# Whole fp32 products for two pairs at each FFN entry, and forget sums by one scan, in a two-layer hybrid trunk

## The chip, the cores and the metric

The kernel is one program on one core of one Trainium2 chip. The metric is the device time of a launch in microseconds. Before the change it is 2557.03 us, the median of three runs (2553.33 to 2557.09).

## The reference

Two layers, each FFN, mixer, FFN, with an RMS norm before and after each part. 512 rows of a prompt and 8 × 16 rows of samples go through together as 640 tokens of width 1024; the hidden width of an FFN is 2816.

```
h = _rmsnorm(x, g[0]);  gate, up = split(h @ w_in);  x += 0.5 * _rmsnorm((silu(gate) * up) @ w_out, g[1])   # four FFNs
# even mixer, attention branch (8 heads of 64), with a cumulative log forget
logf = log_sigmoid(f_logit + b_f)
c_all = cumsum(concat([flogf_past, logf], axis=1), axis=1)
s = einsum('bqhd,bkhd->bhqk', q, k_all) + c_q[..., None] - c_keys
s = where(causal, s, -1e30);  y = einsum('bhqk,bkhd->bqhd', softmax(s), v_all)
```

The even mixer has a recurrent branch too (a convolution, gates, a linear scan); the odd mixer is differential attention. Everything is fp32.

## The kernel before

**The input projection of an FFN.** The 2816 hidden units are 22 pairs of a gate block and an up block (`KF` = 22). A pair's block is cut in four quarters, and the transposed tokens in four (512 rows of K by 320 tokens), and the product is formed by a seven-product scheme: P1 and P2 take weights as they were loaded, P5, P6, P7 and P3 take sums of quarters (`s1`, `s2`, `s3`, `s4`, formed in place in the weight buffers by VectorE, L624 to L648), and on the token side P5, P6, P7 and P4 take differences T1 to T4 (`dve_t1`, L749, and `dve_t`, L764, written over the tokens' quarters in `xs`). That makes 154 products per FFN. Each is 4 chunks of K.

**The split.** fp32 operands are written as a high and a low part in the rounded format fp32r, and a product is three matmuls per chunk, low × high, high × low, high × high, 12 in all (L933 to L935; for pair 0, L924, L925 and L929, with the low token part last). ScalarE writes a weight quarter's high part (`act_operand`, L604), VectorE the low part (`dve_operand`, L611), into a ring of 5 places (`w_all`) after 4 places of its own (`w_apart`) for an FFN's first products. The seven token matrices are split once per FFN into `xb`, high by ScalarE (L729), low by VectorE (L733).

**What follows a product.** The seven results of a pair are summed in PSUM and by copies: ScalarE copies P1 (L665), then u2 after P6 (L670) and u3 after P7 (L675); VectorE adds P2 (c11, L695), c22 (L698) and c12 after P3; ScalarE makes silu (L682); VectorE multiplies after P4 (hid1, L702) and the upper half at last (hid2). P6 of a pair waits on TensorE for the P1 copy, P7 for u2, P4 for u3, P3 for c22.

**The order.** The table `SEQUENCE` gives the products' order. TensorE walks through it; ScalarE and VectorE walk through the same table in loops over i (`act_ffn`, `dve_ffn`), each step holding a split of product i and what follows product i − 5, so the table sets the order of their queues too. At an FFN's start TensorE holds P1 0, P1 1, P2 0, then transposes of token tile 3, P2 1, tile 4 and so on (`pe_xt`, L1310), while the norm of tiles 3 and 4 (VectorE L1217) is still running. `X_FRONT` says at which steps the later token matrices are split. SP's queue loads the weights (L385): a buffer of pair j + 3 may be overwritten when P3 of pair j has been split (`sp_unit`).

**The forget sums.** `pe_cumulate` (L2208) makes the cumulative sums per row by products with a triangular matrix: 10 fp32 matmuls of 8 columns. In the attention of the prompt, each head's keys need the same sums spread over all rows: `sums(h)` (L1898) does it again with 10 fp32 matmuls of 128 columns. In the profile an fp32 matmul has two records.

## Time and profile before

| | |
|---|---|
| median of three runs | 2557.03 us |
| the profiled execution | 2557.7 us, its span 2555.5 us, granted clock 0.983 |
| busy: TensorE, its weight loads | 95%, 85% |
| busy: VectorE, ScalarE | 66%, 47% |
| busy: GpSimd | 5% |

The page is of one execution. TensorE's busy time is modelled, so it is read by the starts of its instructions rather than by their lengths: in a stream, the distance from one start to the next is the time that one costs. The entries of the four FFNs begin at 20.08, 818.44, 1267.28 and 2107.03 us.

### The profile page before, as it was taken

To read this page: it belongs to the slowest core of one execution; us is meant where nothing else is said; L and a number is where in the kernel's file an instruction comes from. 1 tells how busy PE (TensorE), PEld (TensorE's weight loads), DVE (VectorE), ACT (ScalarE), POOL (GpSimd) and SP (SyncE) were. 2 spreads that over 40 slices of the span, in tenths; PEclk is the share of its full clock that TensorE was granted. 3 is DMA by queue.
4 is the path that set the end of the run, shared out by engine and by line. 5 is a ranking of instruction groups with operands and counts; after the bars stand their busy time and mean duration, and the time that the engine had idled before them with its cause. 6 is when DMAs were issued, how large, how long until landed. Compare 5 with 4: busy or idle time off the path is not lost.

```text
span 2555.5 us, 37705 instructions
## 1 busy us (share of the span) xinstructions
PE 2424.2 (95%) x13907; PEld 2172.0 (85%) x13907; DVE 1694.6 (66%) x2817; ACT 1207.7 (47%) x2243; POOL 121.7 (5%) x177
## 2 busy tenths in 40 slices
PE   6999999999999899999989999999989798999998
PEld 6999987987777899987789998787777577999887
DVE  7777647666666877755687775563236868777546
ACT  5554435344445555434555553453224755545444
POOL 1000001100002000001100000110000010000000
PEclk8999999999999999999999999999997999999999
DMA  5233335421303223334423333343244042333335
GB/s 144 80 88 83 105 126 164 114 72 52 109 24 122 70 83 83 90 125 132 158 73 83 83 88 127 132 149 118 88 124 116 9 140 67 83 91 92 108 128 177
DMA packets 259139, 261.89 MB, mean 102 GB/s; under 512 B 25567, under 2 KB 213999, under 8 KB 258976
## 3 DMA queue, kind: packets, MB, share of 16 engines
q1 hardware_dynamic: 254224, 243.83, 31.9%
q0 software_dynamic: 4464, 14.80, 1.7%
q8 instruction: 102, 1.67, 0.3%
q10 hardware_dynamic: 288, 1.10, 0.1%
q14 instruction: 61, 0.50, 0.1%
HBM read 249.11 MB, written 10.58 MB: 102 GB/s over the span
## 4 chain that ended last, share of the span: by engine, by line
PE 79%; DVE 13%; ACT 3%; issue 3%; DMA 1%; POOL 1%; SPq 0%; DVEq 0%; ACTq 0%; POOLq 0%
PE ps L933 13%; PE ps L935 13%; PE ps L934 13%; PE ps L991 5%; PE ps L992 5%; PE ps L993 5%; PE ps L1420 3%; PE ps L1422 3%; PE ps L1421 3%; PE ps L1050 2%; PE ps L1052 2%; PE ps L1051 2%; DVE w_all L611 1%; DVE xb L733 1%; DVE small L2033 1%
## 5 line engine op out<-in xcount | busy, mean ns | idle before, releaser
L933 PE MATMUL ps<-xb,w_all 128*128 128x320 f32 x2320 | 722.2, 311 | 24.0 <-DVE arena L702 11.2
L934 PE MATMUL ps<-xb,w_all 128*128 128x320 f32 x2320 | 720.0, 310 | 0.0
L935 PE MATMUL ps<-xb,w_all 128*128 128x320 f32 x2320 | 719.9, 310 | 0.0
L933 PEld LDWEIGHTS ps<-xb,w_all 128*128 128x128 f32 x2320 | 438.8, 189 | 29.4 <-DVE w_all L611 16.9
L511 DVE TENSOR_TENSOR w_all<-raw,w_all 128x1024 fp32r<-128x1024 f32 (+1 forms) x204 | 208.1, 1020 | 364.2 <-ACT w_all L521 196.9
L934 PEld LDWEIGHTS ps<-xb,w_all 128*128 128x128 f32 x2320 | 438.6, 189 | 0.0
L935 PEld LDWEIGHTS ps<-xb,w_all 128*128 128x128 f32 x2320 | 438.3, 189 | 0.0
L505 ACT ACTIVATE w_all<-raw 128x1024 fp32r<-128x1024 f32 (+1 forms) x204 | 182.5, 895 | 442.2 <-PE ps L993 237.5
L611 DVE TENSOR_TENSOR w_all<-raw,w_all 128x512 fp32r<-128x512 f32 x404 | 278.1, 690 | 150.6 <-ACT w_all L604 149.8
L604 ACT ACTIVATE w_all<-raw 128x512 fp32r<-128x512 f32 x404 | 253.6, 629 | 197.4 <-PE ps L935 134.8
L991 PE MATMUL ps<-w_all 128*128 128x512 f32 x528 | 205.9, 390 | 0.9 <-DVE w_all L526 0.9
L992 PE MATMUL ps<-w_all 128*128 128x512 f32 x528 | 205.5, 389 | 0.0
L993 PE MATMUL ps<-w_all 128*128 128x512 f32 x528 | 205.4, 389 | 0.0
L611 DVE TENSOR_TENSOR w_all<-gain,w_all 128x512 fp32r<-128x512 f32 x196 | 135.0, 690 | 70.3 <-ACT w_all L604 69.7
L604 ACT ACTIVATE w_all<-gain 128x512 fp32r<-128x512 f32 x196 | 122.9, 629 | 87.8 <-PE ps L935 68.1
L1420 PE MATMUL ps<-w_all,xT_lo 128*128 128x512 f32 x354 | 142.1, 401 | 14.8 <-ACT tok L1488 8.3
L1421 PE MATMUL ps<-w_all,xT_hi 128*128 128x512 f32 x354 | 138.2, 390 | 0.0
L1422 PE MATMUL ps<-w_all,xT_hi 128*128 128x512 f32 x354 | 138.0, 390 | 0.0
L991 PEld LDWEIGHTS ps<-w_all 128*128 128x128 f32 x528 | 99.1, 188 | 23.2 <-DVE w_all L526 2.6
L993 PEld LDWEIGHTS ps<-w_all 128*128 128x128 f32 x528 | 99.1, 188 | 20.7
L992 PEld LDWEIGHTS ps<-w_all 128*128 128x128 f32 x528 | 99.1, 188 | 20.1
L1420 PEld LDWEIGHTS ps<-w_all,xT_lo 128*128 128x128 f32 x354 | 66.6, 188 | 37.6 <-DVE w_all L511 17.2
(375 smaller groups left out, 4075.2 us busy)
## 6 DMA issues: line engine op xcount, KB each, us to landing
raw<-in_w_ffn_out SPq DMA_DIRECT2D x176, 512.0 KB, 3.3
raw<-in_w_ffn_in SPq DMA_DIRECT2D x120, 512.0 KB, 5.1
gain<-in_w_ffn_in SPq DMA_DIRECT2D x56, 512.0 KB, 4.3
raw<-in_w_in_odd SPq DMA_DIRECT2D x56, 256.0 KB, 2.7
raw<-in_w_out_even SPq DMA_DIRECT2D x16, 512.0 KB, 3.4
raw<-in_w_out_odd SPq DMA_DIRECT2D x16, 512.0 KB, 3.5
gain<-in_norm_g POOLq DMA_DIRECT2D x12, 512.0 KB, 6.3
raw<-in_w_in_even SPq DMA_DIRECT2D x24, 256.0 KB, 2.7
```

Source lines behind the costliest of these rows:

```text
L511: return nc.vector.tensor_tensor(lo, raw[:, RAW[u][0], 0:n], hi.bitcast(F32), ALU.subtract)
L604: nc.scalar.activation(w_ring(i)[0], operand_raw(f, name, j), ACT.Copy).then_inc(op_hi, 1)
L611: nc.vector.tensor_tensor(lo, operand_raw(f, name, j), hi.bitcast(F32), ALU.subtract).then_inc(op_lo, 1)
L933: nc.tensor.matmul(dst, wl, xh[:, k, :], start=fresh and k == 0, stop=False, skip_group_check=True)
L934: nc.tensor.matmul(dst, wh, xl[:, k, :], start=False, stop=False, skip_group_check=True)
L935: mm = nc.tensor.matmul(dst, wh, xh[:, k, :], start=False, stop=(k == HK - 1), skip_group_check=True)
L991: nc.tensor.matmul(dst, xl, wh[:, cols], start=start, stop=False)
L992: nc.tensor.matmul(dst, xh, wl[:, cols], start=False, stop=False)
L993: mm = nc.tensor.matmul(dst, xh, wh[:, cols], start=False, stop=stop)
L1420: nc.tensor.matmul(dst, xl, wh, start=(k == 0), stop=False)
L1421: nc.tensor.matmul(dst, xh, wl, start=False, stop=False)
L1422: return nc.tensor.matmul(dst, xh, wh, start=False, stop=(k == KD - 1))
```

## The change

**Whole products (the FFNs).** `WHOLE = 2`: the 14 products of pairs 0 and 1 in each FFN are plain fp32 matmuls, one per chunk, with the weight buffers and the token quarters as they are. They wait for the loaded weights, the sums and the T's themselves (`pe_whole_ready`) rather than for splits. The T's are written into the low places of `xb` as fp32 (`xb_f32`), so they no longer go over the tokens; s2 of the two pairs is written to two places of the ring (`whole_s2`). The splits of T1 to T4 and B22, which pair 2 and the rest need, move to steps 14 to 21. `SEQUENCE` has a new beginning (26 products, the same from P1 of pair 4 on), the transposes of tiles 3 and 4 stand together before P2 of pair 1, pair 0's first sums go between the norms of tiles 3 and 4, and the weight buffers of pairs 0 and 1 come free with the product P3 itself.

**Forget sums (the even mixer).** Four transposes put the negated log forgets of all heads as 8 rows of 512 into PSUM, VectorE makes one scan along them (`c_rows`), four transposes turn it back for the row sums, and `sums(h)` is one fp32 product of 512 columns that spreads row h to all 128 rows.

```diff
-SEQUENCE = [("P1", 0), ("P1", 1), ("P2", 0), ("P2", 1), ("P1", 2), ("P2", 2)]
-SEQUENCE += [(name, j) for name in ("P5", "P6", "P7", "P4", "P3") for j in range(2)]
-SEQUENCE += [("P5", 2), ("P1", 3), ("P6", 2), ("P2", 3), ("P7", 2), ("P5", 3), ("P4", 2), ("P6", 3), ("P3", 2), ("P7", 3)]
-SEQUENCE += [(name, j - back) for j in range(4, KF + 1)
+SEQUENCE = [("P1", 0), ("P2", 0), ("P1", 1), ("P2", 1), ("P5", 0), ("P1", 2), ("P6", 0), ("P2", 2), ("P7", 0), ("P5", 1)]
+SEQUENCE += [("P4", 0), ("P6", 1), ("P3", 0), ("P7", 1), ("P5", 2), ("P4", 1), ("P6", 2), ("P3", 1), ("P7", 2)]
+SEQUENCE += [(name, j - back) for j in range(3, KF + 1)
              for name, back in (("P1", 0), ("P5", 0), ("P4", 1), ("P6", 0), ("P2", 0), ("P3", 1), ("P7", 0))
              if j - back < KF]
...
+WHOLE = 2
+SPLIT = [i for i, (_, j) in enumerate(SEQUENCE) if j >= WHOLE]
...
+                i = PLACE["P3", (prev - UNITS["A%d" % f]) // 2]
+                if i in SPLIT_NO:
+                    sp.wait_ge(op_lo, split_count(f, i))
+                else:
+                    sp.wait_ge(prod_mm, NPROD * f + i + 1)
...
 
             a11, a12, a21, a22 = quarters(f, j)
             g = KF * f + j
-            dve.wait_ge(op_lo, NPROD * f + PLACE["P1", j] + 1)
+            operand_free(dve, f, "P1", j)
             pair_wait(dve, f, j, 1)
             nc.vector.tensor_tensor(a11, a11, a21, ALU.subtract).then_inc(s3_done, 1)
...
         def dve_sums(dve, f, i):
 
             name, j = SEQUENCE[i]
...
-            if (name, j) == ("P4", 1):
-                dve_first_sums(dve, f, 2)
-            if name == "P1" and j >= 3:
+            if name == "P1" and j > WHOLE:
                 dve_first_sums(dve, f, j)
-            if name == "P5" and j >= 2:
+            if name == "P5" and j >= WHOLE:
                 dve_s2(dve, f, j)
-            if name == ("P7" if j < 2 else "P5" if j < 4 else "P2"):
-                dve.wait_ge(op_lo, NPROD * f + PLACE["P2", j] + 1)
-                dve.wait_ge(s2_done, KF * f + j + 1)
-                nc.vector.tensor_tensor(a12, a12, a21, ALU.subtract).then_inc(s4_done, 1)
+            if j >= WHOLE and name == ("P5" if j == WHOLE else "P2"):
+                dve_s4(dve, f, j)
 
```

The token matrices, the loops and the products:

```diff
+        def x_whole(name):
+
+            return xb_f32[:, XB[name] + 1] if name in T_NO else xs_quarter(*XB_AT[name])
 
         def act_xb(act, f, name):
...
         def dve_xb(dve, f, name):
+
+            if name in T_NO:
+                dve.wait_ge(prod_mm, done_of(f, {x: p for p, x in XOF.items()}[name], WHOLE - 1))
             dve.wait_ge(xb_hi_done, 7 * f + XB_ORDER.index(name) + 1)
-            nc.vector.tensor_tensor(xb[:, XB[name] + 1], xs_quarter(*XB_AT[name]), xb[:, XB[name]].bitcast(F32),
+            nc.vector.tensor_tensor(xb[:, XB[name] + 1], x_whole(name), xb[:, XB[name]].bitcast(F32),
                                     ALU.subtract).then_inc(xb_lo_done, 1)
 
         def dve_t1(dve, f, t):
...
+            t1 = nc.vector.tensor_tensor(x_whole("T1")[:, :, c0:c1], b12, xs[:, 0:HK, c0:c1], ALU.subtract)
             if t == NT - 1:
...
-            nc.vector.tensor_tensor(xs_quarter(*out), xs_quarter(*plus), xs_quarter(*minus),
-                                    ALU.subtract).then_inc(t_add, 1)
+                dve.wait_ge(t_add, 4 * f + T_NO["T2"])
+            nc.vector.tensor_tensor(x_whole(name), plus, minus, ALU.subtract).then_inc(t_add, 1)
...
         def dve_first_t(dve, f):
 
-            dve_first_sums(dve, f, 0)
-            dve_t1(dve, f, 2)
-            dve_t1(dve, f, 3)
-            dve_operand(dve, f, 4)
-            dve_operand(dve, f, 5)
-            dve_t1(dve, f, 4)
-            dve_operand(dve, f, 6)
-            dve_first_sums(dve, f, 1)
-            dve_xb(dve, f, "T1")
-            dve_t(dve, f, "T3")
-            dve_operand(dve, f, 7)
-            dve_t(dve, f, "T2")
+            for t in range(2, NT):
+                dve_t1(dve, f, t)
 
         FFN_A = ["A0", "A1", "A2", "A3"]
...
         THIRD_LATE = PLACE["P4", 0] + RING + 1
-        X_FRONT = {8: "T2", 10: "T3", 12: "T4", 14: "B22"}
...
                     dve_xb(dve, f, X_FRONT[i])
-                if 7 < i < NPROD:
+                if i in SPLIT_NO:
                     dve_operand(dve, f, i)
-                if i in (6, 7):
-                    dve_s2(dve, f, i - 6)
-                elif 9 < i < NPROD:
                     dve_sums(dve, f, i)
+                if i == 5:
+                    dve_t(dve, f, "T2")
+                if i == 6:
+                    dve_s2(dve, f, 0)
+                if i == 7:
+                    dve_t(dve, f, "T3")
+                if i == 8:
+                    dve_first_sums(dve, f, 1)
+                    dve_s2(dve, f, 1)
                 if i == 9:
                     dve_t(dve, f, "T4")
+                    dve_s4(dve, f, 0)
+                if i == 11:
+                    dve_s4(dve, f, 1)
+                if i == 13:
+                    dve_first_sums(dve, f, WHOLE)
                 if 0 <= i - RING < NPROD and i - RING != THIRD[1]:
...
 
+        def pe_whole_ready(pe, f, name, j):
+
+            g = KF * f + j
+            if name in ("P1", "P2"):
+                pair_wait(pe, f, j, 0)
+            elif name == "P4":
+                pair_wait(pe, f, j, 1)
+            else:
+                pe.wait_ge({"P5": s1_done, "P6": s2_done, "P7": s3_done, "P3": s4_done}[name], g + 1)
+            if XOF[name] in T_NO:
...
-                if i == AHEAD - 1:
+                if i == PLACE["P2", 1]:
                     pe_xt(pe, pre_, 3, 3)
-                if i == AHEAD:
                     pe_xt(pe, pre_, 4, 4)
-
-                    pe.wait_ge(xt_hi, XT[pre_] + 4)
-                if i == AHEAD + 2:
+                if i == PLACE["P5", 0]:
                     pe.wait_ge(xt_hi, XT[pre_] + NT)
-                pe.wait_ge(op_lo, NPROD * f + i + 1)
-                if j == 0:
-                    pe.wait_ge(xb_hi_done, 7 * f + XB_ORDER.index(XOF[name]) + 1)
+                if j < WHOLE:
+                    pe_whole_ready(pe, f, name, j)
+                else:
+                    pe.wait_ge(op_lo, split_count(f, i))
...
                 dst = bank({"P2": b2, "P5": b5, "P3": b5}.get(name, b1), HT)
-                hi, lo = w_ring(i)
...
-                if j == 0:
-
+                if j < WHOLE:
+                    w = whole_s2(j) if name == "P6" else operand_raw(f, name, j)
                     for k in range(HK):
-                        wh, wl = hi[:, k * P:(k + 1) * P], lo[:, k * P:(k + 1) * P]
-                        nc.tensor.matmul(dst, wl, xh[:, k, :], start=fresh and k == 0, stop=False, skip_group_check=True)
-                        nc.tensor.matmul(dst, wh, xh[:, k, :], start=False, stop=False, skip_group_check=True)
-                    pe.wait_ge(xb_lo_done, 7 * f + XB_ORDER.index(XOF[name]) + 1)
-                    for k in range(HK):
-                        wh = hi[:, k * P:(k + 1) * P]
-                        mm = nc.tensor.matmul(dst, wh, xl[:, k, :], start=False, stop=(k == HK - 1), skip_group_check=True)
```

The entry's norms, and the forget sums:

```diff
             f = FFN_PRE.get("pre%d" % (p + 1))
-            if f is not None:
-                for i in range(2):
-                    dve_operand(dve, f, i)
-            elif nxt:
+            if nxt:
                 for i in range(2):
...
             if f is None and nxt:
...
-            if f is not None:
-                dve_operand(dve, f, 3)
             pre(dve, p, 3)
             if f is None:
                 dve_lo(dve, nxt[0] + 3, None, nxt[1]).then_inc(lo_done, 1)
+            else:
+                dve_first_sums(dve, f, 0)
             pre(dve, p, 4)
...
                     pe.wait_ge(nc_done, h)
-                for kb in range(NP):
-                    for b in range(kb + 1):
-                        mm = nc.tensor.matmul(bank(6, P, kb * P), lgn[:, b, h:h + 1].to_broadcast([P, P]),
-                                              con[:, C_UT:C_UT + P] if b == kb else ones,
-                                              start=(b == 0), stop=(b == kb))
-                mm.then_inc(nc_mm, 1)
+                nc.tensor.matmul(bank(6), con[0:NH, C_ID + h:C_ID + h + 1].to_broadcast([NH, P]), c_rows,
+                                 start=True, stop=True).then_inc(nc_mm, 1)
...
             for i in range(NP):
-                for b in range(i + 1):
-                    mm = nc.tensor.matmul(bank(7, NH, 64 + i * NH), con[:, C_UT:C_UT + P] if b == i else ones,
-                                          lgf[:, b, :], start=(b == 0), stop=(b == i))
+                mm = nc.tensor.transpose(ps[0:NH, 7, i * P:(i + 1) * P], lgn[:, i, :], ident)
+            mm.then_inc(lg_ps, 1)
+
+        def pe_cumulate_turn(pe):
+            pe.wait_ge(cum_done, 1)
+            for i in range(NP):
+                mm = nc.tensor.transpose(bank(7, NH, 64 + i * NH), c_rows[:, i * P:(i + 1) * P],
+                                         con[0:NH, C_ID:C_ID + NH])
             mm.then_inc(cq_mm, 1)
 
...
+                pe_cumulate_turn(pe)
...
                 if m == K_AT + 2:
-                    dve.wait_ge(cq_mm, 1)
-                    nc.vector.tensor_copy(cq, bank(7, NP * NH, 64).rearrange("p (t h) -> p t h", h=NH)).then_inc(cq_done, 1)
+                    dve.wait_ge(lg_ps, 1)
+                    nc.vector.tensor_tensor_scan(c_rows, con[0:NH, C_ONE:C_ONE + 1].to_broadcast([NH, SEQ]),
+                                                 ps[0:NH, 7, :], 0.0, ALU.mult, ALU.add).then_inc(cum_done, 1)
...
                     dve_sample_prepare(dve, 0)
+            dve.wait_ge(cq_mm, 1)
+            nc.vector.tensor_scalar(cq, bank(7, NP * NH, 64).rearrange("p (t h) -> p t h", h=NH),
```

The following rows are the order of instructions on an engine: line, operation, written from read, and what it waits for. Lines of the changed kernel have moved: L611 is L637 there, L604 L630, L665 L701, L670 L706, L675 L711, L682 L718, L764 L801, L749 L789, L695 L731, L1898 L1920.

VectorE at the first FFN's entry, before, from the first sums of pair 0 on (`op_hi` is a split's high part, `xt_hi` a transposed token tile, `t_add` a finished T):

```order
L624 TENSOR_TENSOR raw<-raw 128x512 [waits raw_in2,op_lo]
L626 TENSOR_TENSOR raw<-raw 128x512 [waits s3_done]
L749 TENSOR_TENSOR arena<-arena 128x4x64 [waits xt_hi,xb_lo_done]
L749 TENSOR_TENSOR arena<-arena 128x4x128 [waits xt_hi]
L611 TENSOR_TENSOR w_all<-gain,w_all 128x512 [waits op_hi] x2
L749 TENSOR_TENSOR arena<-ps,arena 128x4x128 [waits xt_ps]
L611 TENSOR_TENSOR w_all<-raw,w_all 128x512 [waits op_hi]
L624 TENSOR_TENSOR raw<-raw 128x512 [waits raw_in3,op_lo]
L626 TENSOR_TENSOR raw<-raw 128x512 [waits s3_done]
L733 TENSOR_TENSOR xb<-arena,xb 128x1280 [waits xb_hi_done]
L764 TENSOR_TENSOR arena<-arena 128x4x320 [waits xt_hi,t_add]
L611 TENSOR_TENSOR w_all<-raw,w_all 128x512 [waits op_hi]
```

The same place in the changed kernel; its first sums of pair 0 (L657, L659) stand ahead of it:

```order
L789 TENSOR_TENSOR xb_f_50<-arena 128x4x64 [waits xt_hi]
L789 TENSOR_TENSOR xb_f_50<-arena 128x4x128 [waits xt_hi]
L789 TENSOR_TENSOR xb_f_50<-ps,arena 128x4x128 [waits xt_ps]
L637 TENSOR_TENSOR w_apart<-gain,w_apart 128x512 [waits op_hi]
L801 TENSOR_TENSOR xb_f_50<-arena,xb_f_50 128x1280 [waits t_add,xt_hi]
L667 TENSOR_TENSOR w_f_58<-raw 128x512 [waits s3_done]
L731 TENSOR_TENSOR scratch<-scratch,ps 128x320 [waits prod_mm,p1_done]
L637 TENSOR_TENSOR w_apart<-gain,w_apart 128x512 [waits op_hi]
L801 TENSOR_TENSOR xb_f_50<-arena 128x1280
L657 TENSOR_TENSOR raw<-raw 128x512 [waits raw_in3,prod_mm]
L659 TENSOR_TENSOR raw<-raw 128x512 [waits s3_done]
L667 TENSOR_TENSOR w_f_58<-raw 128x512 [waits s3_done]
```

The split of T1 (L733) and the splits of the ring's first places are gone from between the T's, s2 and the c11 sum stand where they were, and pair 1's first sums come after T3.

ScalarE at the same place before, from the first silu (L682) to u2 of pair 0 (L670), after the copies of P1:

```order
L682 ACT_TABLE_LOAD
L682 ACTIVATE scratch<-scratch 128x320 [waits c11_done]
L729 ACTIVATE xb<-arena 128x1280 [waits t_add]
L604 ACTIVATE w_all<-raw 128x512 [waits prod_mm,s3_done]
L682 ACTIVATE scratch<-scratch 128x320 [waits c11_done]
L604 ACTIVATE w_all<-raw 128x512 [waits prod_mm,s3_done]
L729 ACTIVATE xb<-arena 128x1280 [waits t_add]
L604 ACTIVATE w_all<-raw 128x512 [waits prod_mm,raw_in2]
L670 ACTIVATE scratch<-ps 128x320 [waits prod_mm]
```

And changed, from the copy of P1 of pair 0 (L701) to u2 and u3 of pair 0 (L706, L711):

```order
L701 ACTIVATE scratch<-ps 128x320 [waits prod_mm]
L630 ACTIVATE w_apart<-gain 128x512 [waits raw_in4]
L701 ACTIVATE scratch<-ps 128x320 [waits prod_mm]
L630 ACTIVATE w_apart<-gain 128x512 [waits raw_in4]
L718 ACT_TABLE_LOAD
L718 ACTIVATE scratch<-scratch 128x320 [waits c11_done] x2
L706 ACTIVATE scratch<-ps 128x320 [waits prod_mm]
L711 ACTIVATE arena<-ps 128x320 [waits prod_mm]
```

Pair 0's u2 copy (L706) stood behind both silu and the splits between them; now it stands right behind the two silu, which wait for c11 of pairs 0 and 1, and no split stands between.

TensorE in the prompt's attention before, around the sums of the second head (`nc_done` is the copy of the sums before them, `s_read` the reading of a score block):

```order
L1919 MATMUL ps<-arena 128x384 [waits hl_copied]
L1898 MATMUL ps<-con,arena 128x128 [waits nc_done]
L1898 MATMUL ps<-con,arena 128x128 x9
L1694 MATMUL ps<-con,scratch 128x128 [waits sn_done]
L1694 MATMUL ps<-con,scratch 128x128 x3
L1919 MATMUL ps<-arena 128x512 [waits s_read]
```

And changed:

```order
L1939 MATMUL ps<-arena 128x384 [waits hl_copied]
L1920 MATMUL ps<-arena,con 128x512 [waits nc_done]
L1718 MATMUL ps<-con,scratch 128x128 [waits sn_done]
L1718 MATMUL ps<-con,scratch 128x128 x3
L1939 MATMUL ps<-arena 128x512 [waits s_read]
```

The ten matmuls of 128 columns are one of 512; nothing else moved.

## Rows read from the trace of the kernel before

**Rows 1.** The page: the chain that ended last, share of the span by engine.

```profile
PE 79%; DVE 13%; ACT 3%; issue 3%; DMA 1%; POOL 1%; SPq 0%; DVEq 0%; ACTq 0%; POOLq 0%
```

**Rows 2.** Timeline of PE (start, us): first product, P1 of pair 4, by FFN.

```profile
20.08 0.60 PE L924 MATMUL ps<-xb,w_apart 128*128 128x320 f32 x1 [0.82 <-ACT xb L729]
...
83.25 0.31 PE L933 MATMUL ps<-xb,w_all 128*128 128x320 f32 x1
...
818.44 0.31 PE L924 MATMUL ps<-xb,w_apart 128*128 128x320 f32 x1
...
882.37 0.31 PE L933 MATMUL ps<-xb,w_all 128*128 128x320 f32 x1
...
1267.28 0.30 PE L924 MATMUL ps<-xb,w_apart 128*128 128x320 f32 x1
...
1330.07 0.31 PE L933 MATMUL ps<-xb,w_all 128*128 128x320 f32 x1
...
2107.03 0.30 PE L924 MATMUL ps<-xb,w_apart 128*128 128x320 f32 x1
...
2170.08 0.31 PE L933 MATMUL ps<-xb,w_all 128*128 128x320 f32 x1
```

**Rows 3.** Timeline of PE: two successive steady products' first matmuls.

```profile
150.13 0.31 PE L933 MATMUL ps<-xb,w_all 128*128 128x320 f32 x1
...
151.89 0.31 PE L933 MATMUL ps<-xb,w_all 128*128 128x320 f32 x1
```

**Rows 4.** Timeline of PE: the longest waits of the second FFN's entry.

```profile
842.53 0.42 PE L924 MATMUL ps<-xb,w_all 128*128 128x320 f32 x1 [2.99 <-DVE w_all L611]
...
864.92 0.38 PE L933 MATMUL ps<-xb,w_all 128*128 128x320 f32 x1 [2.87 <-DVE arena L702]
```

**Rows 5.** Timeline of PE: fp32 matmuls of the even mixer.

```profile
543.92 1.02 PE L2281 MATMUL ps<-arena 128*128 128x512 f32 x2
...
544.78 0.38 PE L2282 MATMUL ps<-arena 128*128 128x128 f32 x2
```

**Rows 6.** Weight loads of a product (busy us, mean ns, idle before).

```profile
L933 PEld LDWEIGHTS ps<-xb,w_all 128*128 128x128 f32 x2320 | 438.8, 189 | 29.4 <-DVE w_all L611 16.9 <-issue 12.5
```

**Rows 7.** Windows: length, busy (count) of PE PEld DVE ACT POOL, PEclk.

```profile
43.00:50.00 7.00, 6.52 (x26) 6.53 (x27) 7.00 (x10) 6.99 (x11) 0.00 (x0) 0.53 0.00 1
```

**Rows 8.** Groups by form in 813 to 865: VectorE, then ScalarE.

```profile
L611 DVE TENSOR_TENSOR w_all<-raw,w_all 128x512 fp32r<-128x512 f32 x12 | 8.0, 684 | 1.4 <-ACT w_all L604 1.4
...
L604 ACT ACTIVATE w_all<-raw 128x512 fp32r<-128x512 f32 x13 | 8.0, 623 | 5.7 <-DMA raw<-in_w_ffn_in 5.6
```

**Rows 9.** Timeline of PE and VectorE: tiles 3 and 4 of the second FFN.

```profile
826.12 1.09 PE L1310 MATMUL ps<-con,tok 128*128 128x128 f32 x8 [0.95 <-DVE tok L1217]
...
826.97 0.39 PE L933 MATMUL ps<-xb,w_apart 128*128 128x320 f32 x1
...
826.78 1.28 DVE L1217 SCALAR_TENSOR_TENSOR tok<-x,small,gain 128x1024 f32<-128x1024 f32 x1 [0.72 <-POOL small L1186]
```

**Rows 10.** Timeline of SP's queue: pair 3's weights of the second FFN.

```profile
854.66 4.07 SPq L385 DMA_DIRECT2D raw<-in_w_ffn_in  x4
```

**Rows 11.** Timeline of PE: first head's sums; a later head of the loop.

```profile
677.94 3.86 PE L1898 MATMUL ps<-con,arena 128*128 128x128 f32 x20
...
702.80 2.50 PE L1898 MATMUL ps<-con,arena 128*128 128x128 f32 x20
...
706.28 1.12 PE L1919 MATMUL ps<-arena 64*128 64x512 f32 x2
...
711.84 0.82 PE L1898 MATMUL ps<-con,arena 128*128 128x128 f32 x5
```

**Rows 12.** Windows (columns as in rows 7): eight heads of the attention loop.

```profile
684.30:756.00 71.70, 69.77 (x446) 52.72 (x444) 51.10 (x158) 36.07 (x102) 0.00 (x0) 1.00 0.03 9
```

**Rows 13.** Groups by form in 600 to 640: old cumulate; recurrence scan.

```profile
L2208 PE MATMUL ps<-small,con 128*128 128x8 f32 x20 | 2.3, 252 | 0.0
...
L2393 DVE TENSOR_TENSOR_SCAN att<-att 128x640 f32<-128x640 f32 x1 | 1.5, 1492 | 0.0
```

More of the change, by code:

```diff
@@ L130 @@
 PLACE = {key: i for i, key in enumerate(SEQUENCE)}
+WHOLE = 2
+SPLIT = [i for i, (_, j) in enumerate(SEQUENCE) if j >= WHOLE]
+SPLIT_NO = {i: n for n, i in enumerate(SPLIT)}
+NSPLIT = len(SPLIT)
 RING, AHEAD = 5, 4
@@ L178, in build_trunk @@
         att = at_byte("att", 0, [P, 3456], back=4 * (W_ALL - 4 * BW))
+        w_f32 = at_byte("w_f32", 0, [P, W_ALL], back=4 * W_ALL)
         gain = at_byte("gain", 8 * D, [P, 2, D])
@@ L371, in build_trunk, with split_count @@
         O_BANK = [0, 1, 4, 3, 2]
+        def split_count(f, i):
+            return NSPLIT * f + SPLIT_NO[i] + 1
         def sp_unit(sp, u, it, src):
@@ L1146, in act_norm_rest @@
             sq_m(act, p, 4)
-            if f is not None:
-                for i in range(2, AHEAD):
-                    act_operand(act, f, i)
             if p == 5:
@@ L1164, in act_norm_start @@
                 sq_x(act, -1, t)
-            act_operand(act, 0, 0)
             for t in TILES[0]:
                 act_xt(act, "pre0", t, t)
-            act_xb_first(act, -1)
-            for i in range(1, AHEAD):
-                act_operand(act, 0, i)
             for t in TILES[1]:
                 sq_x(act, -1, t)
+            act_xb_first(act, -1)
             act.wait_ge(lam_sum, 1)
@@ L1243, in dve_norm_rest @@
             f = FFN_PRE.get("pre%d" % (p + 1))
-            if f is not None:
-                for i in range(2):
-                    dve_operand(dve, f, i)
-            elif nxt:
+            if nxt:
                 for i in range(2):
@@ L1252, in dve_norm_rest @@
             post_gain(dve, p, 4)
-            if f is not None:
-                dve_operand(dve, f, 2)
             if f is None and nxt:
@@ L1259, in dve_norm_rest @@
                 return
-            if f is not None:
-                dve_operand(dve, f, 3)
             pre(dve, p, 3)
@@ L1276, in dve_norm_start @@
                 pre(dve, -1, t)
-            dve_operand(dve, 0, 0)
-            dve_xb_first(dve, -1)
-            for i in range(1, AHEAD):
-                dve_operand(dve, 0, i)
             dve.wait_ge(par_in, 16 * 9)
```

83 lines of the change are left out of this document (52 added, 31 removed).

## The prediction

> **What bounds the kernel now.** I began with the chain of work that ended last: TensorE carries most of it and VectorE is a distant second [rows 1]. So a time is won where TensorE stops or where it is given fewer columns, and I looked for its stops. The timeline of TensorE through the four FFNs shows two regimes. In the steady one a product of the input projection takes 151.89 − 150.13 = 1.76 us with nothing between products [rows 3]; nothing the change does to VectorE or ScalarE can help there. In the entry it is otherwise. From the first product to the start of P1 of pair 4 lie 26 products, which would take 26 × 1.76 = 45.8 us, and the rows give 63.17, 63.93, 62.79 and 63.05 us, 252.9 in all and 63.2 in the mean [rows 2]. Two groups of eight transposes belong there (826.97 − 826.12 = 0.85 each [rows 9]), 1.7. The remaining 15.7 us of each entry are waits and stretches at a low clock: four times that, 63 us, is all that the FFN part can draw on. The longest waits are 2.99 us for an operand split by VectorE (L611) and 2.87 us for a multiplication of VectorE (L702) [rows 4]: TensorE waits for its preparers.
>
> **What a whole fp32 product costs.** The trace has no whole product in the FFN, but it has fp32 matmuls in the even mixer: two records of 512 columns (L2281) start at 543.92 and the next line at 544.78, so 0.43 us a record [rows 5]. Per column that is 0.84 ns, and 320 columns take 0.27. A whole product has 4 chunks of 2 records: 8 × 0.27 = 2.15 us, against 1.76 for the 12 split matmuls. The change thus makes 14 products per FFN longer by 0.39, 5.5 us per FFN, 22 in four. This is the price; the rest must be earned by waits that go.
>
> What can make a record longer is its weight load. A load takes 189 ns [rows 6], and 12 of them, 2.27 us, are more than the 1.76 of a product [rows 3]; so loads lie beside the matmuls before them. A 0.27 us record has more room for its load than a 0.147 us one, and I add nothing. The Trainium skill speaks against that: "TensorE: Matmul & The Clock Gate", Part 3, "The mechanism", says a weight load overlaps running matmuls only where it goes to another row group, and every load here takes all 128 rows. By that rule a record would take 0.46, a product 3.67; the rows just named do not bear the rule out, so it gets a small chance among the rivals.
>
> **What the entry gives back.** Per FFN, 14 splits go on ScalarE (0.62 each) and 14 on VectorE (0.68 each) [rows 8]: 18 us of preparing, in queues that serve a TensorE that waits. The splits of T1 to T4 and of B22 don't go, they move behind the first 14 places; T1 can be used as soon as it is written. So the 2.99 us stop, whose last link was a split, has no place any more. The 2.87 us stop stands at the end of a transfer: SP issues pair 3's weights at 854.66, they take 4.07 us to land [rows 10], the first sums of pair 3 stand on them in VectorE's queue and L702 stands behind these. The new order has P3 of pair 0 as product 12 instead of 14, and the buffer is freed by the product itself. I put that issue at 850.3 in the second FFN, so the weights land about 854.4, while P1 of pair 3 comes at place 19, about 863. That stop goes too.
>
> What is late next I worked out by laying the second FFN out, each engine's queue in the order shown ahead, with durations of the rows. Three stops remain.
> - Transposes of token tile 4. Both late tiles are now transposed before P2 of pair 1. TensorE is through three whole products at 818.44 + 3 × 2.15 = 824.9 and through tile 3 at 825.8. Tile 4 is normalised by VectorE from 826.78 to 828.06 now [rows 9]; four splits (2.7 us) leave the queue ahead of it, and pair 0's two first sums (1.4, of a split's shape) enter, so it is done about 827.5: a wait of 1.7.
> - P7 of pair 0 needs the copy of P6's result (u2). On ScalarE this copy stands behind both silu of pairs 0 and 1, as it did, and the second waits for VectorE's sum after P2 of pair 1, which comes late in that engine's queue, about 838.5, behind T3 and the first sums of pair 1. The copy is done at 839.5, TensorE there 1.2 earlier.
> - P7 of pair 2 needs a copy that waits for the last hidden block of pair 0, VectorE's at 861.0: a wait of 1.3.
>
> Together 4.2 us. The entry is then 14 × 2.15 + 12 × 1.76 + 1.7 + 4.2 = 57.1 instead of 63.2, a gain of 6.1 and **24.5 us** in four FFNs (5.6 in the first, where the first products run at the low clock and the whole products pay double for it, but start 1.0 earlier as they wait for no split; 6.7, 6.3 and 5.9 in the others). Its bounds: with no stop left the gain is 4 × 10.3 = 41; with every stop of before still there it is a loss of 22, the price alone. I stay near the first end since the two longest stops have links that are simply no longer there.
>
> The clock enters here too. In the first FFN from 43 to 50 us the granted clock is 0.53, the lower level of 1.2 GHz, and 26 matmuls fill 6.52 us [rows 7], after a stop of 3 us. At that level a whole product would be 4.3 us. Fewer long stops before means fewer such stretches; I book no extra gain for it, since the sum already ran at full pitch save in the first FFN.
>
> **The forget sums.** In the prompt's attention each head begins with 20 records of 128 columns (L1898): 2.50 us, and 3.86 for the first head [rows 11]. The new product has one row set of 8 partitions against 512 columns, two records; a 512-column fp32 product of this same loop takes 1.12 [rows 11]. Saved are 1.38 per head, 7 heads 9.7, and 2.7 for the first: 12.4 if all of it falls on the stream. In the loop TensorE is busy 69.77 of 71.70 us and VectorE 51.10, ScalarE 36.07 [rows 12], so TensorE sets the pace, but a head of 711.84 − 702.80 = 9.04 us will come down to 7.8 with some 6.4 of VectorE in it (51.10 / 71.70 of 9.04), and the chain of scores, exponent, transposes has less slack. I take **11**, the lower end being only the first head's 2.7, where the loop comes to be set by that chain.
>
> The other half is a wash. The 20 records of the old cumulate (2.3 us busy [rows 13]) go; 4 transposes come in their place and 4 later, each time half of the 0.85 for eight [rows 9], and one scan over 512 columns on VectorE: the scan in the recurrence takes 1.49 for 640 [rows 13], so about 1.2. It lies beside the projection's matmuls, with the transposes back at the start of the Q part, many microseconds on. At worst TensorE waits there for the scan, 1.2; at best it saves 1.4. I take 0.
>
> **The sum.** 2557.0 − 24.5 − 11 = 2521.5. The profiled run of before took 2557.7 (its span is 2555.5), 0.7 over the median, so differences from its rows stand on the median unscaled. Forecast **2522**.
>
> **Rivals.**
> - *The stops return* (0.20). VectorE and ScalarE are in-order queues, and some ten operations change places on each. If one late link costs each entry 3.5 us more (a u2 copy behind a silu, first sums behind a transfer, a low-clock stretch at 4.3 per product for two products), the FFN part is 10: 2557 − 10 − 11 = 2536. For it: two of my three remaining stops hang on such copies. Against it: their total work has fallen by 18 us per entry.
> - *The attention loop isn't TensorE's* (0.10). If the chain between engines sets a head's 9.04 us, only the first head's gain stays: 2557 − 24.5 − 2.7 = 2530. For it: the loop has waits between every two engines. Against it: 97% busy at a granted clock of 1.00 [rows 12].
> - *Weight loads are laid bare* (0.04), the slower end. If the 189 ns load of a whole record can't be hidden (fp32 weights, unlike the split ones), a record is 0.27 + 0.19 = 0.46, a product 3.67, and 56 products cost 85 us more than in my sum. The longer products would swallow the 4 × 4.2 = 17 of stops, so the time is 2522 + 85 − 17 = 2590. It decides from 35 us more, that is 2.15 + 35 / 56 = 2.8 us per whole product, 0.35 a record. Against it: rows 3 and 6 above, and the 0.43 per record in rows 5, which is no more than twice the pitch of a split matmul scaled to 512 columns (1.76 / 12 × 1.6 × 2 = 0.47, from rows 3) and leaves room for no bare load.
> - *Nothing much* (0.04): the FFN part at 0 from stops and clock together and the loop kept by its chain, 2557 − 2.7 = 2554.
>
> **How the numbers follow.** The forecast has 0.62, the rest above 0.38. Its own range is 2510 to 2531 (waits 1.5 to 6 per entry, attention 9 to 12). The range for 8 in 10 reaches on the fast side to all stops gone with the whole of the forget sums, 2557 − 41 − 12.4 = 2504, and on the slow side to the first rival and a little of the second with it, 2543. A measurement of this kernel tells 0.2%, about 5 us, from no change. Faster: forecast and the first two rivals, 0.92; within 0.2%: 0.04; slower: 0.04.
>
> **What would show it.** A whole product in the trace after should start 2.15 us before the next, its records 0.27 apart. The four entries, first product to P1 of pair 4, should be 56 to 58 us, with stops at the tile 4 transposes and before P7 of pairs 0 and 2, and none near 3 us. A head of the attention loop should be 7.8 us. An entry above 60 says the stops returned, a product above 2.8 that the loads are bare, a head still at 9 that another chain sets the loop. The prediction is wrong if whole products run at the lower clock for several pairs, as then each costs 4.3 and ten of them eat the FFN gain.

## The result

The changed kernel takes 2564.28 us (median of six runs, 2561.65 to 2567.31) where the kernel before takes 2555.31 (six runs): a ratio of 1.0033, with an interval of 1.0022 to 1.0045. It is slower by 9.0 us, little but clear of the noise; a gain of 35 us was forecast. The profiled run, the fastest of the six, has a span of 2559.7 us, 4.2 more than the profiled run of before; the trace can account for these 4.2 only.

The FFN entries did what the prediction said. On the timeline of TensorE in the changed kernel, the first whole product and the start of P1 of pair 4 in each FFN (start, us, engine, line, operation, count), answering to [rows 2]:

```profile
18.86 0.54 PE L966 MATMUL ps<-arena,raw 128*128 128x320 f32 x1
...
77.00 0.31 PE L973 MATMUL ps<-xb,w_all 128*128 128x320 f32 x1
...
841.36 0.43 PE L966 MATMUL ps<-arena,raw 128*128 128x320 f32 x1
...
898.24 0.31 PE L973 MATMUL ps<-xb,w_all 128*128 128x320 f32 x1
...
1283.11 0.43 PE L966 MATMUL ps<-arena,raw 128*128 128x320 f32 x1
...
1339.97 0.31 PE L973 MATMUL ps<-xb,w_all 128*128 128x320 f32 x1
...
2117.30 0.43 PE L966 MATMUL ps<-arena,raw 128*128 128x320 f32 x1
...
2174.29 0.31 PE L973 MATMUL ps<-xb,w_all 128*128 128x320 f32 x1
```

The entries are 58.14, 56.88, 56.86 and 56.99 us, 228.9 together: 24.1 less than the 252.9 of before. And yet the second FFN begins at 841.36 instead of 818.44. The loss lies between the first FFN's entry and that start. The same timeline at the loop over the heads, the spread of the sums (L1920) of four of its heads, answering to [rows 11]:

```profile
676.85 1.12 PE L1920 MATMUL ps<-arena,con 8*128 8x512 f32 x2
...
684.29 1.12 PE L1920 MATMUL ps<-arena,con 8*128 8x512 f32 x2
...
697.10 2.07 PE L1920 MATMUL ps<-arena,con 8*128 8x512 f32 x2
...
711.28 2.07 PE L1920 MATMUL ps<-arena,con 8*128 8x512 f32 x2
```

From the second head's sums to the third's it is 684.29 − 676.85 = 7.44 us. That can't be held against the 7.8 of the forecast, which was for a steady head: the same step took 8.42 us before, and only the next ones 9.04.

```profile
685.34 2.50 PE L1898 MATMUL ps<-con,arena 128*128 128x128 f32 x20
...
693.76 2.50 PE L1898 MATMUL ps<-con,arena 128*128 128x128 f32 x20
```

Then a head of the changed kernel takes 711.28 − 697.10 = 14.18, and the two records that took 1.12 take 2.07. The windows say why (length, busy time and count of TensorE, weight loads, VectorE, ScalarE and GpSimd, then the granted clock and DMA), first of before, then of after:

```profile
680.00:760.00 80.00, 78.06 (x485) 59.59 (x484) 54.23 (x165) 38.22 (x106) 1.46 (x3) 0.99 0.08 31
```

```profile
680.00:760.00 80.00, 79.33 (x231) 48.26 (x230) 40.17 (x120) 29.48 (x81) 0.00 (x0) 0.54 0.02 7
...
690.00:700.00 10.00, 10.00 (x29) 6.19 (x29) 5.59 (x18) 2.77 (x8) 0.00 (x0) 0.50 0.00 0
...
700.00:710.00 10.00, 10.00 (x34) 7.15 (x34) 4.89 (x13) 5.09 (x12) 0.00 (x0) 0.50 0.01 2
```

The page shows it at a glance, in the row of the granted clock in 40 slices of 64 us (tenths), at the eleventh and twelfth:

```profile
PEclk9999999999759999999999999999998999999999
```

TensorE is busy all the time, more than before, but with 231 matmuls in the 80 us where there were 485 (in part by the change itself, as a head has 18 records fewer): its granted clock is 0.50 from about 686 on, the lower of its two levels (1.2 GHz), and was 0.99. VectorE and ScalarE, by contrast, have become idler. And no long stop goes ahead of the fall: the longest wait of TensorE in the ten us before it is 0.48 us.

```profile
682.86 0.66 PE L1979 MATMUL ps<-arena,att 128*128 128x64 f32 x4 [0.48 <-ACT att L2008]
```

From the first head's sums to the second FFN it is 172.29 us (841.36 − 669.07) against 140.50 before, 31.8 us lost where 11 were to be won. So the books are: 24.1 won in the entries, 1.2 by the earlier start of the first one, 2.6 between P1 of pair 4 of the first FFN and the loop, 31.8 lost in the loop and behind it, the rest within 0.4: 4.2 slower.

### The profile page after: what moved, and what is told of

Its sections match the earlier page's. It is cut to its first block, busy times and chain, and to the rows that moved or that the text cites. A ratio compares the mean times of both kernels' runs of the same rounds, so it can differ in the third digit from the quotient of the medians.

```text
span 2559.7 us, 36785 instructions
## 1 busy us (share of the span) xinstructions
PE 2456.5 (96%) x13527; PEld 2151.1 (84%) x13527; DVE 1666.6 (65%) x2762; ACT 1180.7 (46%) x2187; POOL 118.5 (5%) x177
## 4 chain that ended last, share of the span: by engine, by line
PE 82%; DVE 11%; ACT 3%; issue 2%; DMA 1%; POOL 1%; ACTq 0%; SPq 0%; DVEq 0%
PE ps L973 13%; PE ps L974 13%; PE ps L975 13%; PE ps L1031 5%; PE ps L1033 5%; PE ps L1032 5%; PE ps L1444 3%; PE ps L1446 3%; PE ps L1445 3%; PE ps L1090 2%; PE ps L1092 2%; PE ps L1091 2%; PE ps L966 2%; PE ps L1939 1%; PE ps L1979 1%
## 5 line engine op out<-in xcount | busy, mean ns | idle before, releaser
L973 PE MATMUL ps<-xb,w_all 128*128 128x320 f32 x2176 | 672.9, 309 | 9.2 <-ACT scratch L706 6.7
L974 PE MATMUL ps<-xb,w_all 128*128 128x320 f32 x2176 | 672.4, 309 | 0.0
L975 PE MATMUL ps<-xb,w_all 128*128 128x320 f32 x2176 | 672.4, 309 | 0.0
L973 PEld LDWEIGHTS ps<-xb,w_all 128*128 128x128 f32 x2176 | 408.4, 188 | 12.0 <-issue 12.0
L974 PEld LDWEIGHTS ps<-xb,w_all 128*128 128x128 f32 x2176 | 408.4, 188 | 0.0
L975 PEld LDWEIGHTS ps<-xb,w_all 128*128 128x128 f32 x2176 | 408.4, 188 | 0.0
L637 DVE TENSOR_TENSOR w_all<-raw,w_all 128x512 fp32r<-128x512 f32 x364 | 251.6, 691 | 144.4 <-ACT w_all L630 143.5
L630 ACT ACTIVATE w_all<-raw 128x512 fp32r<-128x512 f32 x364 | 229.2, 630 | 182.4 <-PE ps L975 138.0
L637 DVE TENSOR_TENSOR w_all<-gain,w_all 128x512 fp32r<-128x512 f32 x180 | 124.4, 691 | 65.3 <-ACT w_all L630 64.9
L630 ACT ACTIVATE w_all<-gain 128x512 fp32r<-128x512 f32 x180 | 113.4, 630 | 84.1 <-PE ps L975 66.2
```

What stands on the lines that cost most here:

```text
L630: nc.scalar.activation(w_ring(i)[0], operand_raw(f, name, j), ACT.Copy).then_inc(op_hi, 1)
L637: nc.vector.tensor_tensor(lo, operand_raw(f, name, j), hi.bitcast(F32), ALU.subtract).then_inc(op_lo, 1)
L973: nc.tensor.matmul(dst, wl, xh[:, k, :], start=fresh and k == 0, stop=False, skip_group_check=True)
L974: nc.tensor.matmul(dst, wh, xl[:, k, :], start=False, stop=False, skip_group_check=True)
L975: mm = nc.tensor.matmul(dst, wh, xh[:, k, :], start=False, stop=(k == HK - 1), skip_group_check=True)
```

## Theories

**R**: the clock fell because of the form of the new sums, which put data on 8 of the array's 128 rows where the old ones filled all. **W**: it fell because a head has less matmul work, whatever its form. **S**: it fell by the way the loop is entered (scan and transposes, an earlier start). **H**: the level that the first heads get is kept to the end.

## The two parts by themselves

The FFN part alone, the forget sums as they were:

```diff
-                nc.tensor.matmul(bank(6), con[0:NH, C_ID + h:C_ID + h + 1].to_broadcast([NH, P]), c_rows,
-                                 start=True, stop=True).then_inc(nc_mm, 1)
+                for kb in range(NP):
+                    for b in range(kb + 1):
+                        mm = nc.tensor.matmul(bank(6, P, kb * P), lgn[:, b, h:h + 1].to_broadcast([P, P]),
+                                              con[:, C_UT:C_UT + P] if b == kb else ones,
+                                              start=(b == 0), stop=(b == kb))
+                mm.then_inc(nc_mm, 1)
...
```

> The FFN part alone; the forget sums are as before (20 records of 128 columns per head, old cumulate). The trace after shows the four entries 24.0 us shorter and the attention loop of the even mixer at half the clock. If the loss lies in the sums alone, the loop keeps a granted clock of 1.00 and 9.04 us a head, and the time is 2555 - 24 = 2531 us. If the shorter entries themselves cost something elsewhere, it is above 2540.

2530.62 us (2528.24 to 2531.05), a ratio of 0.9898 (0.9881 to 0.9914): 25.7 us won against the 2556.31 that the kernel before took beside it, as expected. The loop's window in that run, at 9.04 us a head, shows the upper level:

```profile
700.00:710.00 10.00, 10.00 (x65) 7.54 (x63) 7.21 (x20) 5.81 (x15) 0.00 (x0) 1.00 0.15 52
```

The forget part alone, on the FFNs of before:

> The forget part alone, the FFNs as before. If the loss lies in it, the loop runs at a granted clock near 0.5 with about 14.2 us a head, and the time is 2555 + 29 = 2584 us. If the loop fell to the low clock only because it starts some 9 us earlier behind the new FFN entry, the clock here stays at 1.00 and the time is about 2543.

2591.08 us (2587.23 to 2591.94), 1.0138 (1.0121 to 1.0155): 34.8 us lost, where 29 were expected, with the loop low as in the changed kernel. So the entries, and the start that they move, have no part in it. The two parts add up to the whole: 34.8 − 25.7 = 9.1 us, and 9.0 were measured.

```profile
696.00:716.00 20.00, 20.00 (x59) 12.46 (x57) 9.89 (x30) 7.02 (x20) 0.00 (x0) 0.50 0.00 0
```

Then the forget part was split in its turn: sums as before, the scan and its transposes kept.

> The changed kernel with each head's sums as before (20 records of 128 columns); the scan and the two groups of four transposes stay. It prices the cumulate part, which the prediction put at 0 between -1.4 and +1.2. Between the first FFN's entry and the loop the trace of after is 2.8 us shorter than before, so theory R expects the loop at 1.00 with 9.04 us a head and 2530.6 - 2.8 = 2528 us. Theory S (the scan and its transposes bring the loop in at the low clock) expects 0.5 and above 2560.

2530.65 us (2529.06 to 2531.55), the same as without the scan. Theory S falls, and so does the 2.8 us that the two traces had seemed to show for the scan: the first head's sums start at 671.92 here and at 671.97 in the FFN part alone. The loop's start moves by as much without a cause in the program: two kernels below, with the changed kernel's instructions up to the loop, enter it at 671.28 and 671.91, and the changed kernel at 669.07. So the 2.6 us of the books can't be put down to the change either. The scan took 1.20 us on VectorE and its transposes 0.6 and 0.4 us busy, and they are worth what they cost.

## Rows or work

One difference to the changed kernel: the selector and the sums take all 128 rows. Rows 8 to 127 meet zeros of the selector, so the sums are the same.

```diff
-                nc.tensor.matmul(bank(6), con[0:NH, C_ID + h:C_ID + h + 1].to_broadcast([NH, P]), c_rows,
+                nc.tensor.matmul(bank(6), con[:, C_ID + h:C_ID + h + 1].to_broadcast([P, P]), c_all,
```

> The changed kernel with one difference: the product that spreads a head's sums takes all 128 rows of the array (the selector's other rows are zero) instead of 8, still 512 columns and two records. Theory R (the clock fell since the sums no longer fill the array's rows): the loop is granted 1.00, a head takes about 7.5 us, and the time is 2564 - 44 = 2520 us. Theory W (it fell since a head has fewer matmul columns and instructions) and theory S (it fell by the way the loop is entered, whatever the sums look like): 0.5 as in the changed kernel, 14.2 us a head, 2564.

2524.94 us (2524.74 to 2525.84), 0.9879 (0.9863 to 0.9896): 39 us faster than the changed kernel, by rows that add nothing to the result, and 5.7 faster than the FFN part alone. The second and the third head still take 8.63 and 9.62 us, then the clock is back. A later head, from its sums to the next, and three windows:

```profile
695.82 1.12 PE L1921 MATMUL ps<-arena,con 128*128 128x512 f32 x2
...
703.49 1.12 PE L1921 MATMUL ps<-arena,con 128*128 128x512 f32 x2
```

```profile
680.00:690.00 10.00, 9.18 (x31) 5.62 (x30) 6.41 (x21) 4.70 (x14) 0.00 (x0) 0.68 0.00 0
...
690.00:700.00 10.00, 10.00 (x53) 6.48 (x52) 7.31 (x23) 5.62 (x17) 0.00 (x0) 0.98 0.00 1
...
700.00:710.00 10.00, 9.78 (x50) 6.20 (x49) 8.44 (x26) 5.70 (x15) 0.00 (x0) 1.00 0.16 54
```

A head is then 703.49 − 695.82 = 7.67 us (the next takes 8.71 at 1.00, with waits for ScalarE). What rows 8 to 127 bring to the product are gate weights left there by the recurrent branch, so this run doesn't tell filled rows from the numbers in them. The opposite edit keeps the 8 rows and restores the work, by issuing each head's sums three times:

```diff
+                for again in range(3):
+                    mm = nc.tensor.matmul(bank(6), con[0:NH, C_ID + h:C_ID + h + 1].to_broadcast([NH, P]), c_rows,
+                                          start=True, stop=True)
```

> The changed kernel with each head's sums issued three times over, on 8 rows: 6 records of 512 columns, 2.6 us at the full clock, as long on TensorE as the 20 records of before. Theory R: the loop stays near 0.5 and each head gets 4 more records of about 1 us, 18 us a head, time 2564 + 29 = 2593. Theory W: the clock is back at 1.00, a head 9.2 us, time 2534. Theory S: as theory R.

2590.83 us (2589.94 to 2592.11). After its second head the loop is at 0.50 again, to about 814 us:

```profile
716.00:736.00 20.00, 20.00 (x52) 11.14 (x50) 7.66 (x21) 5.68 (x14) 0.00 (x0) 0.50 0.08 26
```

So theory W, as put, falls too: as long on TensorE as before, but on 8 rows, it is no help; as short as in the changed kernel, but on 128 rows, it is.

A third kernel made only 2 of the 8-row product's 512 columns for heads 2 to 7, which then add stale sums.

> The changed kernel without the spread of the sums for heads 2 to 7: only 2 of the 512 columns are made, so these heads add stale sums. It asks whether the 8-row product itself takes the clock down or whether it is the filled rows of before that are missed. If they are missed: 0.5 as in the changed kernel, about 12.2 us a head, 2564 - 6 x 2 = 2552 us. If the 8-row product is the brake: 1.00, about 6.6 us a head, 2564 - 6 x 7.6 = 2518.

2554.49 us in the median, but the seven runs lie in two groups, 2538.68 to 2542.27 and 2554.49 to 2557.30. The profiled one, of the lower group, held 1.00 for two heads longer than the changed kernel and then fell:

```profile
690.00:700.00 10.00, 10.00 (x61) 7.20 (x60) 8.85 (x30) 6.18 (x18) 0.00 (x0) 1.00 0.00 0
...
710.00:720.00 10.00, 10.00 (x33) 6.83 (x33) 4.87 (x15) 3.65 (x10) 0.00 (x0) 0.50 0.00 0
```

So the loop falls without the 8-row product too: something of the old sums is missed, whatever the new product does. The upper group lies near the 2552 that was expected for that case. Whether the 8-row product pulls the clock down besides is not shown: the lower group would fit that, but the next runs fall at different heads with 128-row products as well.

## Does the level follow the rows at once?

Heads 0 to 3 on 128 rows and heads 4 to 7 on 8, and the reverse (`few = h < 4`):

```diff
+                few = h >= 4
+                sel = con[0:NH if few else P, C_ID + h:C_ID + h + 1].to_broadcast([NH if few else P, P])
+                nc.tensor.matmul(bank(6), sel, c_rows if few else c_all, start=True, stop=True).then_inc(nc_mm, 1)
```

> The changed kernel with the sums of heads 0 to 3 on all 128 rows and of heads 4 to 7 on 8 rows, 512 columns in two records throughout. Theory R: the clock is 1.00 (7.7 us a head) while the rows are filled and falls to 0.5 (14.2 us a head) within a head or two after the change, about 2525 + 3 x 6.5 = 2545 us. Theory H (a loop that has got the full clock keeps it, and the 8 rows hurt only at the loop's start): 1.00 to the end, 2525.

> The reverse: heads 0 to 3 on 8 rows, heads 4 to 7 on 128. Theory R: 0.5 in the first heads, back to 1.00 within a head or two after the change, about 2564 - 3 x 6.5 = 2545 us. Theory H: 0.5 to the end, 2564.

The medians are near what R gives, 2548.02 and 2549.80, but the runs spread over 19 and 20 us (2544.57 to 2563.77, 2534.75 to 2554.60), and the traces say that R in its plain form is too simple. In the first one, whose profiled run is the slowest of its eight (2563.77), the clock had fallen by the third head's sums and did not come back, though the third's and the fourth's were on 128 rows (the fifth's, below, are the first on 8):

```profile
685.38 2.08 PE L1923 MATMUL ps<-arena,con 128*128 128x512 f32 x2
...
699.38 2.07 PE L1923 MATMUL ps<-arena,con 128*128 128x512 f32 x2
...
713.38 2.07 PE L1923 MATMUL ps<-arena,con 8*128 8x512 f32 x2
```

In the second it came back, but only after the sums on 128 rows had begun at 713.50, more than two heads earlier:

```profile
713.50 2.08 PE L1923 MATMUL ps<-arena,con 128*128 128x512 f32 x2
```

```profile
730.00:740.00 10.00, 10.00 (x36) 7.15 (x34) 4.81 (x15) 4.35 (x12) 0.00 (x0) 0.50 0.00 0
...
740.00:750.00 10.00, 10.00 (x39) 6.24 (x38) 5.14 (x17) 3.59 (x11) 0.00 (x0) 0.71 0.01 2
...
750.00:760.00 10.00, 10.00 (x56) 6.74 (x55) 8.36 (x28) 6.21 (x19) 0.00 (x0) 1.00 0.00 0
```

H in its plain form falls by the same rows. What the runs show together: where the sums were on 8 rows, every trace fell from 1.00 within two heads and stayed low as long as they were; with the 20 old records every trace was at 1.00 from the second head to the last; with single products on 128 rows both levels occurred with the same instructions, each for two heads or more. What in the old sums holds the level (filled rows, the numbers in them, the number of records, and how much of each) these runs don't separate, and I leave that open.

## Looking for a better kernel

Three more stops of the entry are of the kind that an order can mend: before P2 of pair 1 (transposes and 1.0 us of waiting), before P7 of pair 0 and before P7 of pair 2. The waits of TensorE in the second FFN's entry of the changed kernel, by line (total, times, longest):

```profile
PE ps L973 <- ACT scratch L706: 1.5, 1, 1.5
PE ps L1334 <- DVE tok L1248: 1.0, 1, 1.0
PE ps L966 <- ACT scratch L706: 0.7, 1, 0.7
```

The two that wait for L706, the u2 copy, were attacked by moving three operations ahead (`U2_EARLY` is P6 of pair 0, whose u2 copy goes one step up, `HID_EARLY` P3 of pair 0, the split of B22 goes behind the u2 copy of pair 2), in a kernel with 128-row sums and in one with the old sums:

```diff
-                if i in X_FRONT:
+                if i in X_FRONT and X_FRONT[i] != "B22":
                     act_xb(act, f, X_FRONT[i])
...
+                if i == U2_EARLY + RING - 1:
+                    act_after(act, f, U2_EARLY)
+                if i in X_FRONT and X_FRONT[i] == "B22":
+                    act_xb(act, f, X_FRONT[i])
...
+                    if i == HID_EARLY + RING + 2:
+                        dve_up(dve, f, HID_EARLY)
                     dve_sums(dve, f, i)
```

> The sums on 128 rows, and the two stops that the FFN entries still have before P7 of pairs 0 and 2 attacked: ScalarE's u2 copy of pair 0 goes ahead of the second silu, VectorE's last hidden block of pair 0 ahead of pair 3's first sums, and ScalarE's u2 copy of pair 2 ahead of the split of B22. In the trace of after these stops take 1.28 and 2.03 us in the first FFN, 0.8 and 1.65 to 1.89 in the others, 11.1 in all. If they go and nothing else turns late, 2525 - 11 = 2514 us; if the next link is as late, 2525.

> The new FFN entries with the early copies, the forget sums wholly as before, so that the loop is steady at 1.00. It prices the early copies by themselves: the two stops took 11.1 us in the trace of after, the kernel with the new FFN alone 2530.6. If both stops go: 2519.5. The 128-row pair of kernels gave only 5.4 for it in the median, in a loop whose clock varied; if that is the true price, 2525.

With 128-row sums: 2519.56 us, between 2514.49 and 2527.90. With the old sums: 2516.73 (2515.77 to 2519.27), a ratio of 0.9853 (0.9837 to 0.9869), 13.9 us under the FFN part alone, where 11.1 were expected (about 13 if each is held against the kernel before as measured beside it). In its trace the wait for the tile 4 transposes is the only one left in the second FFN's entry:

```profile
815.38 1.09 PE L1339 MATMUL ps<-con,tok 128*128 128x128 f32 x8 [1.01 <-DVE tok L1253]
```

and the entries are 55.5, 54.3, 54.2 and 54.5 us, together 10.4 less than in the changed kernel (where the rest was won isn't shown). One of them is 861.20 − 806.87:

```profile
806.87 0.43 PE L971 MATMUL ps<-arena,raw 128*128 128x320 f32 x1
...
861.20 0.31 PE L978 MATMUL ps<-xb,w_all 128*128 128x320 f32 x1
```

Two kernels tried to hold the loop's level and keep short sums. One had the old sums in heads 0 to 2 and 128-row products after:

> As the last kernel (sums on 128 rows, early copies), but heads 0 to 2 spread their sums with the 20 records of before, which held the loop at 1.00 from its second head in every trace that has them. Theory: the loop has two lasting states, and the third and fourth head of the 128-row kernel ran at the low one (8.6 and 9.6 us). With the first heads at 1.00 the rest, on 128 rows, stays there at 7.7 us a head: three heads pay 1.4 more, about 5 us of low clock go, the median comes to 2514 and the runs lie within 4 us of each other instead of 13. Rival: the 128-row sums don't hold the clock, and it falls after head 3: 2535 or more.

2515.82 us in the median, but two of six runs took 2529.11 and 2530.05. The expected 4 us of spread were 17: the 128-row product doesn't hold the level by itself, the trace has a fall at the sixth head (2.08 us for its two records, after 1.12 in the two heads before). The other issued the 128-row sums twice:

```diff
+                for again in range(2):
+                    mm = nc.tensor.matmul(bank(6), con[:, C_ID + h:C_ID + h + 1].to_broadcast([P, P]), c_all,
+                                          start=True, stop=True)
```

> The 128-row kernel with early copies, each head's sums issued twice over: 4 records of 512 columns, 1.7 us, less than the 2.3 of the 20 old records and twice the single product. Theory: single products on 128 rows leave the loop at the edge of its high state (the clock fell for a head or two in some runs), and work on full rows, needed or not, keeps it there: 1.00 from the second head on in every run, 8.5 us a head, 2515 us with the runs within 4 us of each other. Rival: doubled work only costs its 0.86 us a head and the falls stay, 2519.6 + 7 = 2526 with a spread above 10 us.

2517.33 us (2512.03 to 2521.02). The spread is 9 us, between the two expectations; the profiled run, its fastest, was at 1.00 through all the heads:

```profile
700.00:710.00 10.00, 9.96 (x53) 6.51 (x52) 7.56 (x25) 5.38 (x18) 0.00 (x0) 1.00 0.00 1
...
720.00:730.00 10.00, 10.00 (x51) 6.27 (x51) 7.56 (x26) 5.43 (x17) 0.00 (x0) 1.00 0.00 0
```

Several kernels thus beat both the kernel before and the changed one, by some 1.5% and 1.8%. The best three (2515.8, 2516.7, 2517.3) can't be told apart by their medians; the one with the forget sums left wholly as they were is the steadiest. With the early copies the forget part, in any of its shapes, is worth nothing that shows; without them the 128-row sums were worth 5.7 us (2524.94 against 2530.62, runs that don't overlap).

## Why the prediction was wrong

**What a whole product costs: right.** Two products that follow each other in the changed kernel:

```profile
868.16 0.43 PE L966 MATMUL ps<-xb_f,w_f 128*128 128x320 f32 x1
...
870.31 0.43 PE L966 MATMUL ps<-arena,raw 128*128 128x320 f32 x1
```

2.15 us, as forecast; a record of 0.27 hides its weight load, and the rival of bare loads is out. The Trainium skill's rule in "TensorE: Matmul & The Clock Gate", Part 3, "The mechanism", that a load overlaps only with matmuls of another row group, doesn't hold here: each of these loads goes to all rows. (The same section of the Trainium skill also lets a load into a background weight buffer go ahead of running matmuls; no run here shows that buffer.)

**The entries: right.** 57.1 was forecast, 56.9 to 57.0 came in three of four; 24.5 us were forecast for four, 24.1 stand in the trace and 25.7 in the runs of the FFN part alone. The two stops near 3 us are gone. Of the three that remained, the tile 4 transposes wait 1.04 us (1.7 forecast), and the gaps before P7 of pairs 0 and 2 are 0.8 to 1.3 and 1.7 to 2.0 us (1.2 and 1.3 forecast). The first rival, the stops' return, didn't come.

**The cumulate: right**, at 0.

**The loop: wrong, and this is the step that failed.** "In the loop TensorE is busy 69.77 of 71.70 us [...], so TensorE sets the pace, but a head [...] will come down to 7.8". The size of the cut was right at the clock of before: with 128-row sums a steady head at 1.00 took 7.67 us, so it is TensorE that sets the pace there, and the rival of another chain is out. The step took the granted clock of 1.00 in [rows 12] as a condition that stays when the instructions that stood under it are exchanged. The old sums were the one part of a head that ran 20 full-row records in a stretch; they cost 2.3 us a head and the loop had its upper level with them. I asked which engine sets the pace, and named as a rival that another chain might. I didn't ask what TensorE's own rate would be afterwards. The paragraph on the clock looked at it only as something that stops of TensorE bring about, as in [rows 7], and so only in the FFN; that it can be low in a stage where TensorE never stops was not among the cases. The row that could have warned me was there: 3.86 us for the first head's sums against 2.50 for the others [rows 11], the loop is entered at the low level, and something in it raises the clock. (The first head's saving was priced at 1.12 us for the new product, the full clock; at 669.07 it took 2.07.) The Trainium skill, in "TensorE: Matmul & The Clock Gate", "HAM oscillation — how this bites in real kernels", lays a fall of the clock to idle gaps of the engine. The windows of after disagree: 10.00 of 10.00 us busy at 0.50.

The range ended at 2543 since its slow side was made of stops that return and a little of a loop set by another chain. Either makes the gain smaller; a forget part that comes out below nothing was in neither. For the sums' term the bound from below should have been a loop at the low level: [rows 7] had the price, matmuls at 0.25 us for 0.147, on 9.04 us a head.

## What to carry to other kernels

Where an edit exchanges matmuls in a stage that is bound by TensorE, its new length is the work divided by the clock that the new stage gets, and not by the clock of before: put the low level into the range for the whole stage. Take a product out by its time alone only if the others would hold the level without it; here the matmuls that looked like waste bought the clock for the ones around them, and full rows that add zeros were worth 39 us. And price the halves of a change apart: 25 us of gain lay in this one, under a loss of 35.

## What was not expected of the hardware

TensorE, busy all the time, ran at its lower level for some 90 us: 0.50 from about 686 us to 778 in the changed kernel, and for 128 us with the 8-row sums issued three times. With the same instructions the loop was seen at either level for two heads on end (heads 2 and 3 on 128 rows: 14.0 us a head in one kernel, 9.6 and 7.7 in another that had the same rows up to there), so that runs of one kernel lay up to 20 us apart, where the kernel before and those with the old sums stay within 8 and 4. The four runs of the 128-row kernel by itself lie within 1.1 us, so the same sums were steady in one kernel and not in the next (13 us with the early copies); why isn't shown.
